# Two stacks of two layers on one core: the norm factor applied in PSUM to the first pair of groups, and the output projections' first two groups led through the contraction together

## The reference, cut to what matters

```
u = h * rsqrt(mean(h*h) + 1e-6) * g          # rms_norm
p = u @ w_in                                 # many groups of columns
h = h + mixer(p) @ w_o
u = rms_norm(h, g_ffn)
h = h + ffn(u)                               # first model: conv_glu, D_FF 2816
                                             # second model: relu(u @ w_up)**2 @ w_down, D_FF 4096
```

## Time and profile before

| | us |
|---|---|
| median of 3 runs | 2047.35 (2044.59 to 2056.27) |
| the profiled execution | 2048.42 |
| its span | 2046.5 |
| PE busy | 1883.6 (92%) |
| VectorE busy | 1293.0 (63%) |
| ScalarE busy | 1140.5 (56%) |
| GpSimd busy | 1037.9 (51%) |
| mean granted PE clock | 0.959 of full speed |

### The profile page before, as it was taken

One profiled execution on the slowest core, in us unless ns is written; L12 is line 12 of the kernel. 1 busy time (PEld: TensorE's weight loads), 2 busy tenths in 40 slices (PEclk: granted clock), 3 DMA queues, 4 the chain that ended last, 5 costly groups with the idle time before them and its releaser, 6 DMA issues.

```text
span 2046.5 us, 44566 instructions
## 1 busy us (share of the span) xinstructions
PE 1883.6 (92%) x16390; PEld 1778.9 (87%) x16390; DVE 1293.0 (63%) x1943; ACT 1140.5 (56%) x1924; POOL 1037.9 (51%) x742
## 2 busy tenths in 40 slices
PE   8889889999999889888999999988899998879999
PEld 8778779999999778778999989866899997669999
DVE  3487725669913397824669963476786536777764
ACT  5653455456755654445557755665555457465544
POOL 5663449839986573448929985741200045411000
PEclk9999989999999999979999999997999999779999
DMA  6432015656665432005656664420366653205665
GB/s 208 122 103 71 23 39 158 176 145 186 188 187 164 124 114 74 23 22 154 176 151 179 187 173 133 150 89 21 112 183 202 193 166 113 72 17 154 186 193 173
DMA packets 146922, 271.20 MB, mean 133 GB/s; under 512 B 16433, under 2 KB 16946, under 8 KB 146738
## 3 DMA queue, kind: packets, MB, share of 16 engines
q1 hardware_dynamic: 145296, 264.97, 45.2%
q10 hardware_dynamic: 1442, 3.66, 0.5%
HBM read 267.52 MB, written 1.05 MB: 131 GB/s over the span
## 4 chain that ended last, share of the span: by engine, by line
PE 65%; DVE 15%; ACT 9%; POOL 8%; issue 3%; DMA 0%; ACTq 0%; DVEq 0%; SPq 0%
PE bank L649 63%; POOL ring_split L1317 8%; ACT arena L1351 7%; ACT hi_ring L1351 1%; PE bank L758 1%; DVE arena L1891 1%; DVE u L1961 1%; DVE arena L1890 1%; DVE arena L2062 1%; DVE arena L1975 1%; DVE arena L1974 0%; DVE arena L2109 0%; DVE arena L1973 0%; ACT L1351 0%; DVE arena L2464 0%
## 5 line engine op out<-in xcount | busy, mean ns | idle before, releaser
L1317 POOL TENSOR_TENSOR ring_split<-ring,hi_ring 128x512 fp32r<-128x512 f32 x682 | 969.1, 1449 | 736.7 <-ACT hi_ring L1351 730.9
L1351 ACT ACTIVATE hi_ring<-ring 128x512 fp32r<-128x512 f32 x1002 | 619.3, 630 | 555.1 <-PE bank L649 532.0
L649 PE MATMUL bank<-u_hi,hi_ring 128*128 128x256 f32 (+1 forms) x2480 | 676.1, 285 | 47.3 <-POOL ring_split L1317 39.7
L649 PE MATMUL bank<-u_split,hi_ring 128*128 128x256 f32 (+1 forms) x2480 | 665.4, 281 | 1.6 <-DVE u_split L1966 1.4
L649 PE MATMUL bank<-u_hi,ring_split 128*128 128x256 f32 (+1 forms) x2480 | 665.0, 281 | 0.0
L649 PEld LDWEIGHTS bank<-u_hi,hi_ring 128*128 128x128 f32 (+1 forms) x2480 | 452.3, 188 | 61.8 <-POOL ring_split L1317 41.1
L649 PEld LDWEIGHTS bank<-u_split,hi_ring 128*128 128x128 f32 (+1 forms) x2480 | 452.4, 188 | 4.0 <-DVE u_split L1966 2.4
L649 PEld LDWEIGHTS bank<-u_hi,ring_split 128*128 128x128 f32 (+1 forms) x2480 | 452.2, 188 | 0.9
L1999 DVE TENSOR_TENSOR ring_split<-ring,hi_ring 128x512 fp32r<-128x512 f32 x320 | 215.3, 694 | 111.9 <-ACT hi_ring L1351 108.1
L649 PE MATMUL bank<-arena 64*64 64x64 f32 (+6 forms) x3680 | 240.3, 255 | 14.6 <-DVE arena L2109 9.3
L649 PEld LDWEIGHTS bank<-arena 64*64 64x64 f32 (+3 forms) x3680 | 210.4, 155 | 49.5 <-issue 29.7
(11 more groups left out here) (246 smaller groups left out, 2407.0 us busy)
## 6 DMA issues: line engine op xcount, KB each, us to landing
ring<-in_stream SPq DMA_DIRECT2D x1002, 256.0 KB, 2.8
par<-in_params ACTq DMA_DIRECT2D x3, 637.0 KB, 4.3
h<-in_x SPq DMA_DIRECT2D x4, 256.0 KB, 4.3
cst<-in_cst SPq DMA_DIRECT2D x1, 993.0 KB
out<-h ACTq DMA_DIRECT2D x3, 256.0 KB, 2.8
par<-in_params ACTq DMA_DIRECT2D x1, 633.0 KB, 8.3
out<-h ACTq DMA_DIRECT2D x2, 128.0 KB, 2.3
msk<-in_masks SPq DMA_DIRECT2D x1, 104.0 KB
```

The source lines that it names most:

```text
L649: ins = nc.tensor.matmul(o, l, r, start=start, stop=stop)
L1317: G.tensor_tensor(ring_lo[:, c, :], ring[:, c, :], hi_ring[:, q % HI_RING, :].bitcast(F32), ALU.subtract).then_inc(lo_by_pool, 1)
L1351: return nc.scalar.activation(o, i, f, **kw)
```

## The change

The first pair of groups behind each norm is multiplied by the raw input, h times gain, without the factor. Its high part comes from ScalarE (`raw_high`, in `last_squares`), its low part from VectorE (`raw_low`, in `add_last`), each behind the addition to `h`, in the same `u_hi` and `u_lo` that the normed input takes afterwards. PE runs `project_raw` straight behind the last output group, with the norm total after k = 1. When the factor is there and the first pair's banks are full, VectorE multiplies the banks by it (`rescale`); cq0 and ckv it multiplies into their buffer instead of ScalarE's copy, and in the second model's U it does Relu and factor in one operation for U0 and U1. The second pair of groups (A2 and A3; cq1, kpe and aq; U2 and U3) now goes through the contraction together on the normed input (`project_normed`). A part of the normed input may be written only when PE has used the raw one (`raw_used`), the last when the second bank is full. All squares are summed by VectorE, so that the norm total has two calls, not four. The warming matmuls are gone. The first two groups of WO go through the contraction together (`two_groups`), all four tiles for each k. The weight stream is reordered to fit.

```diff
+                def project_across(place, enter, leave=False, beside=None, with_ones=0):
+                    names = list(dict.fromkeys(n for n, _ in place))
+                    open_ = {n: B.open(pe, n) for n in names}
...
                     for k in range(KD):
                         for w, a in ((0, 0), (1, 0), (0, 1)):
+                            enter(k, w, a)
+                            for t, (n, o) in enumerate(place):
+                                end = k == KD - 1 and a == 1 and t in last
+                                left = leave and a == 1 and t == 3 and k in (0, 1, 3, 5)
+                                mm(open_[n][:, o:o + T], W.block(q + 4 * k + t)[w], u_parts[a][:, k, :], (k, w, a) == (0, 0, 0) and t in first, end,
+                                   full=n if end else None, done=S["raw_used"] if left else None)
                         W.done(q + 4 * k + 3)
+                        if beside:
+                            beside(k)
...
+                def two_groups(open_, name, act, n, ready, first=True, full=()):
+                    q = W.take(name, 4 * n)
+                    for k in range(n):
+                        ready(k)
+                        for t in range(4):
+                            end = k == n - 1 and t % 2 == 1
+                            mm3(open_[t // 2][:, t % 2 * T:(t % 2 + 1) * T], W.block(q + 4 * k + t), cut(act, k), ...)
                         W.done(q + 4 * k + 3)
...
-                norm_total("norm2", squares, 0)
-                project_first(("U0", "U1"), 5, 8)
-                for i in range(2, 22):
+                project_raw(("U0", "U1"), past, lambda k: norm_total("norm2", squares, "sums_ready", past["sums_ready"] + 1) if k == 1 else None)
+                project_normed([("U2", 0), ("U2", T), ("U3", 0), ("U3", T)], 5)
+                for i in range(4, 22):
                     project(f"U{i}", 2, u_parts)
...
+            def raw_high(C, gain, part_):
+                for k in range(part_.start, part_.stop):
+                    ins = A(u_hi[:, k, :], h[:, k, :], ACT.Copy, scale=gain[:, k:k + 1])
+                C.link(ins, S["raw_hi"])
...
                     C.link(A(u_hi[:, part_, :], u[:, part_, :], ACT.Copy), S["u_hi_ready"])
-                    if j > 1:
-                        hi.make(at + HI_RING + j - 1)
+                    hi.make(at + HI_RING + j + 4)
...
+            def raw_low(C, gain, part_, n):
+                dve.wait_ge(S["raw_hi"], past["raw_hi"] + n)
+                for k in range(part_.start, part_.stop):
+                    ins = V.scalar_tensor_tensor(u_lo[:, k, :], h[:, k, :], gain[:, k:k + 1], u_hi[:, k, :].bitcast(F32), ALU.mult, ALU.subtract)
+                C.link(ins, S["raw_lo"])
...
-                    if sums and j in (1, 2):
+                    if j in (1, 2, 4):
                         dve.wait_ge(S["squares_ready"], past["squares_ready"] + 5 * which + j + 1)
+                        add_squares(C, dst, min(j, 3), S["sums_ready"])
...
+                    raw_low(C, gain, part_, 5 * which + j + 1)
...
                 for j in range(n + 1):
                     if j < n:
+                        if j < n - 1:
+                            dve.wait_ge(S["raw_used"], past["raw_used"] + first // 5 * 4 + j + 1)
+                        else:
+                            B.wait(dve, raw_last)
...
-                    if j > 2:
-                        lo.make(at + HI_RING + j - 2)
+                    lo.make(at + HI_RING + j + 3)
+            def rescale(C, B, names):
+                for name in names:
+                    bank = B.wait(dve, name)
+                    C.link(V.tensor_tensor(v3(bank[:, :], 2), v3(bank[:, :], 2), spread(rn[:], 2), ALU.mult), S["raw_scaled"])
...
+                    if i < 2:
+                        bank = B.wait(dve, f"U{i}")
+                        C.link(V.scalar_tensor_tensor(hidden[:, 2 * i:2 * i + 2, :], v3(bank[:, :], 2), 0.0, spread(rn[:], 2), ALU.max, ALU.mult))
+                        B.release(dve, f"U{i}")
```

More of the change, by code:

```diff
@@ L389, in groups2 @@
     g += ["bn", "ln", "mn0", "mn1"]
[L390 removed]
+    g += [*LAST_WO, "U0", "U1", "norm2"] + [f"U{i}" for i in range(2, 16)] + [*LAST_D]
     return g
@@ new lines, in two_groups @@
+                def two_groups(open_, name, act, n, ready, first=True, full=()):
[4 more added lines that the diff above has]
+                            end = k == n - 1 and t % 2 == 1
+                            mm3(open_[t // 2][:, t % 2 * T:(t % 2 + 1) * T], W.block(q + 4 * k + t), cut(act, k), first and k == 0 and t % 2 == 0, bool(full) and end,
+                                full=full[t // 2] if full and end else None)
@@ L1279, in _ @@
                 for half in range(2):
-                    mix_in = after("mix_ready", 2 * half, 2)
-                    for j, (name, part_) in enumerate(zip(LAST_WO, PARTS)):
-                        bank = B.open(pe, name) if half == 0 else banks[B.slot[name][0]]
-                        tiles = part_.stop - part_.start
+                    names = LAST_WO if half else [name + " attention" for name in LAST_WO]
+                    open_ = [B.open(pe, name) if half == 0 else banks[B.slot[name][0]] for name in LAST_WO]
@@ L1284, in _ @@
+                    parts = cut((mix_hi, mix_lo), slice(4 * half, 4 * half + 4))
+                    two_groups(open_[:2], names[0], parts, 4, after("mix_ready", 2 * half, 2), half == 0, LAST_WO[:2] if half else ())
+                    W.ends[names[1]] = W.ends[names[0]]
+                    for j in range(2, len(LAST_WO)):
+                        tiles = PARTS[j].stop - PARTS[j].start
                         for i in range(tiles):
-                            q = W.take(name if half else name + " attention", 4)
+                            q = W.take(names[j], 4)
@@ L1286, in _ @@
                             for k in range(4):
-                                if i == 0 and j == 0:
-                                    mix_in(k)
-                                mm3(bank[:, i * T:(i + 1) * T], W.block(q + k), cut((mix_hi, mix_lo), 4 * half + k), half == 0 and (i, k) == (0, 0),
-                                    (half, i, k) == (1, tiles - 1, 3), full=name if (half, i, k) == (1, tiles - 1, 3) else None)
+                                end = (half, i, k) == (1, tiles - 1, 3)
@@ L1292, in _ @@
+                                mm3(open_[j][:, i * T:(i + 1) * T], W.block(q + k), cut(parts, k), half == 0 and (i, k) == (0, 0), end, full=LAST_WO[j] if end else None)
                                 W.done(q + k)
-                norm_total("norm2", squares, 0)
-                project_first(("U0", "U1"), 5, 8)
-                for i in range(2, 16):
+                project_raw(("U0", "U1"), past, lambda k: norm_total("norm2", squares, "sums_ready", past["sums_ready"] + 1) if k == 1 else None)
```

262 lines of the change are left out of this document (141 added, 121 removed).

## The result

The changed kernel takes 2110.83 us in the median of 4 runs (2103.75 to 2113.27), beside 2049.32 (2044.59 to 2056.27) for the kernel before: a ratio of 1.0292, with a 95% interval of 1.025 to 1.0333. It is slower by 61 us; 2066 was forecast, and its range ended at 2080.

What follows compares the result with a forecast made beforehand. PE (TensorE) was taken to bound the kernel, with about two thirds of the chain that ended last. Losses of 70.4 us against a gain of 51.1 gave +19 on 2047.35, so 2066 us; range 2030 to 2080.

Steps and rivals of the forecast that it cites:

- Gross gain 51.1: Norms, start and first model's output projections: time saved by removed gaps, norm-total calls and warming matmuls, 51.1 us in all.
- what it adds: The forecast's list of added costs, on the way into the raw pair and in the second pair.
- the 0.9 before Sin: Last down projection of the first model: new copies ahead of the table load and Sin cost 0.9 us.
- Six stops, 6 x 1.5 = 9: Stops of 3 us and more (start, A, four U): PE's clock drop costs 1.5 us each, 9 in all.
- The prediction's own other case: Whole kernel: with a clock drop after every stop above 2.5 us, the sum would be 2072 us.
- WO tail 3.6: First model's output projections: 2.9 us idle and 0.7 later for the last pieces, 3.6 each, twice 7.2.
- norm-total wait 6.4: Second model, way into the pair: late piece 3.5 us, then norm total some 2.9 late; 2 x 6.4 = 12.8.
- Pieces 9 to 11 late 15: Second pair: last norm parts and pieces come late, 6.0 us in four norms, 2 and 7 elsewhere, sum 15.
- Piece 12 stands behind the consumers' work: Second pair: piece 12 waits for the first groups' consumers; 4.4 us and 8.4 in the models' U, 7.2 in A.
- rival D: Stops follow one another: second model's norm-total wait drops the clock, VectorE's lag lasts to the down projection; 2085, chance 0.05.

Runs made afterwards that it cites:

- e9: e2 with single output groups and VectorE's angles ahead of its first raw part in the first model's last down projection: 2066.28 us, 1.0073 to the kernel before.
- e3: e2 with one or two more weight pieces made between the addition to h and the raw parts in output and down projections: 2085.01 us, 1.0174.
- e10: Changed kernel with VectorE's raw low parts in output and down projections cut to one column of 256, results left out: 2096.36 us, 1.0225.
- e7: e2 with VectorE, not GpSimd, subtracting weight pieces 8 to 11 of the first model's second pairs: 2078.74 us, 1.0148.
- e2: e1 with both piece makers going two weight pieces further before they take the first pair's results: 2080.13 us, 1.0155.
- e1: Changed kernel with ScalarE's wait for the next layer's parameters moved behind its pieces and first sum-of-squares operation of the down projection: 2109.18 us, 1.0293.
- e14: Kernel before, with only ScalarE's wait for the next layer's parameters added ahead of its down projection pieces: 2062.37 us, 1.0024.
- e8: Kernel before with only the output projections' first two groups paired and no warming matmuls there: 2051.82 us, 1.0012.
- e12: e9 with VectorE adding the next bank to h before the raw steps of the bank before, in output and down projections: 2066.24 us, 1.0075.

## Why the prediction was wrong

The direction was right and so was the mechanism of most terms, and the sum was a third of what came. Two steps failed by most: a wait that was not priced at all, and the clock, which was sized at 9 us and came to over 23. By the steps of the forecast:

- **"Gross gain 51.1."** Held where it can be read: the first pair's end came 3.9 us earlier (5), the norms' gaps are gone, the start of the output projection won 3.3 and not 1.4.
- **What the moved part waits for: put at nothing.** Under "what it adds" the forecast priced the raw copies' operations and not the wait that came with them. It stands ahead of the pieces of a projection that was not under study, and those starts are 14.4 us longer in the trace. In time it was worth 1 to 9 us when put alone into the kernel before. In the same way the 0.9 before Sin priced ScalarE's copies and left out that VectorE's raw part stands ahead of the angles that Sin needs: +4.7, of which e9 took back 3.4.
- **"Six stops, 6 x 1.5 = 9."** The price of one drop was near; the number of stops was not. The slow products of the changed kernel cost 23.5 us more than those before (26 in the second profile). Of that, 6.8 stand in the second model's pairs and 2.1 in the first model's feed-forward pairs, where the forecast had 6, and 2.0 at the start and in the second A, where it had 3. But 3.6 are in the first model's output projections and 2.3 in the second's, where it had none, and 3.9 at the starts of the down projections. The prediction's own other case, a drop after every stop above 2.5 us, gave 2072.
- **"WO tail 3.6" and "norm-total wait 6.4".** The chain to the next piece was right (6.6 us for 6.4, stops of 3.19 and 4.14 for 2.9 and 3.5). The further 2.9 us of idle at the norm total did not come (0.23): in its place 36 products ran at half pace and lost 2.9. That the two sizes are alike is luck. Where e3 and e10 shorten the stop before it, the wait for the total does stand in the trace. From the stop at 1500.67 to the end of the feed-forward groups, each layer of the second model lost 2.5 us more than forecast, 1.0 of it in the late groups. The rest of that row, 1.0 us in each attention half, can't be read: the second profile has it in one layer only.
- **"Pieces 9 to 11 late 15"** was given to GpSimd's hold on VectorE. Its stops came, 1.2 us each and twice in a norm: 9.3 us in the four norms for which 6.0 was forecast. The held operations are as read, and without the hold (e7) these stops are smaller; but the time does not move, since VectorE then has the pieces to make. That the hold alone sets this term is not shown.
- **"Piece 12 stands behind the consumers' work"** is the term that held best: 3.6 to 4.4 us in six pairs, and e2 gave 29 us back where 28 was expected from it.
- Not in the forecast: before, VectorE waited some 0.2 us in each later group of the first model's feed-forward; after, it runs without a pause, as a group of its work takes 5.65 us and so does PE's, so what it is late by in the second pair lasts for 18 groups. They are 3.1 us longer over two layers, and in e1 the stop at the start of D stayed at 3.93 us, not 2.86. This is read from the traces; no kernel tested it alone. It is what rival D said of VectorE's lag.

Of the rivals, D (2085, given 5%) was the nearest. With the parameters' wait and the order before Sin in it, the sum would have been 19 + 14 + 4 = 37 us against the profile's 55; with the clock drops outside those starts as they came (10.6 more than forecast) some 48.

What stays open: why the time of e1 and e14 shows less than the stretches of their traces, how much time the clock's share is worth (it is counted from product starts; no run takes it out by itself), and the part of the 61 us (some 6) by which the medians differ more than the two profiled executions.

## What to carry to other kernels

When a step moves to an earlier place, list what it waits for as well as what it does, and ask what stands behind that wait on its engine: here the gains came by a DMA issued two lines earlier. An engine that feeds a ring a few pieces ahead must make pieces before each long step, and only as many as the ring lets it: two more here gave 29 us, and the same idea one step too far took 6 to 8. A stop in dense matrix work can cost more than its length: count one drop of the clock for each stop of about 3 us and more, those outside the stretch under study too. A gap filled with work that another engine must prepare is no gain if that engine has no slack: as the traces read, the gap's 6 us was VectorE's and ScalarE's time to catch up.

## What the runs showed of the hardware

The steady product has two paces at full granted clock. 576 products of the last down projection take 67.84 us in 13 of the 17 profiles and 65.28 in four (the kernel before, e7, e8, e9), 0.118 and 0.113 each, and nothing between; e9 and e12 do the same work there and differ, and so do the two profiles of the changed kernel in 576 products of its last feed-forward (68.88 and 66.48). The level steps jump by 3 to 4 us too. What selects the pace was not found.
